# Attention closes, swap and peak, and the sample's distance table: three moves in the order of a hybrid decoder step

## The reference

```
h = rmsnorm(x);  proj = h @ w_in
qkv = silu(short_conv(proj[:, :1536]));  q, k = l2norm(q), l2norm(k)
o_a = rmsnorm(gated_delta_rule(q, k, v, g, beta, s0)) * silu(z_a)     # 4 heads of 128, in chunks
o_b = merge(window 128 step 1, window 512 step 4, window 2048 step 16) * silu(z_b)   # 8 heads of 64
y = rmsnorm(x + concat(o_a, o_b) @ w_out)
```

## Time and profile before

| | us |
|---|---|
| median of 3 runs | 1913.91 |
| lowest, highest | 1909.18, 1929.31 |
| the profiled execution | 1917.42 |
| its span | 1915.7 |
| TensorE busy in the span | 1731.0 (90%) |
| VectorE, ScalarE, GpSimd busy | 830.4, 640.2, 370.9 |

### The profile page before, as it was taken

How to read it: one execution, slowest core, us unless ns; L and a number is a source line. 1 busy time by engine, 2 the same in 40 slices (tenths; PEclk the granted TensorE clock), 3 DMA queues, 4 the chain that set the end, 5 groups by cost and what they waited for, 6 DMA issues and landing times. The chain is left out here.

```text
span 1915.7 us, 27681 instructions
## 1 busy us (share of the span) xinstructions
PE 1731.0 (90%) x9686; PEld 1420.9 (74%) x9686; DVE 830.4 (43%) x1913; ACT 640.2 (33%) x1550; POOL 370.9 (19%) x372
## 2 busy tenths in 40 slices
PE   5999999999999999977799899899988578889896
PEld 5998878888888888865688778778876546667674
DVE  3435413522351153127854544444442565445552
ACT  4534312421231132111425445444534223333331
POOL 0000000000000010026132422342243333423321
PEclk9999999999999999989799999999989569899998
DMA  5424677776566877769857457645430486465650
GB/s 171 121 67 100 167 232 217 146 180 236 145 177 203 216 160 154 237 212 290 225 132 194 121 124 158 163 114 122 133 111 15 147 235 190 150 169 171 187 180 27
DMA packets 228267, 311.30 MB, mean 162 GB/s; under 512 B 62973, under 2 KB 176509, under 8 KB 218669
## 3 DMA queue, kind: packets, MB, share of 16 engines
q1 hardware_dynamic: 223540, 301.35, 58.6%
q10 hardware_dynamic: 4608, 8.39, 1.3%
HBM read 229.10 MB, written 147.56 MB: 197 GB/s over the span
## 5 line engine op out<-in xcount | busy, mean ns | idle before, releaser
L399 PE MATMUL pj<-hT_hi,w_hi 128*128 128x512 f32 x896 | 362.5, 405 | 1.8 <-DVE raw L652 1.8
L400 PE MATMUL pj<-hT_lo,w_hi 128*128 128x512 f32 x896 | 355.2, 396 | 0.0
L401 PE MATMUL pj<-hT_hi,w_lo 128*128 128x512 f32 x896 | 354.8, 396 | 0.0
L401 PEld LDWEIGHTS pj<-hT_hi,w_lo 128*128 128x128 f32 x896 | 168.8, 188 | 41.0
L399 PEld LDWEIGHTS pj<-hT_hi,w_hi 128*128 128x128 f32 x896 | 168.9, 188 | 39.8 <-issue 2.1
L400 PEld LDWEIGHTS pj<-hT_lo,w_hi 128*128 128x128 f32 x896 | 169.2, 189 | 37.0
L1483 PE MATMUL o_ps<-pt,vt 128*65 128x256 f32 (+3 forms) x560 | 150.3, 391 | 10.7 <-DVE ot L1749 6.6
L1584 ACT ACTIVATE pt<-pt_ps 128x512 f32<-128x512 f32 x144 | 84.9, 590 | 153.6 <-PE pt_ps L1461 153.5
L2360 PE MATMUL y_bank<-wo_hi,mh 128*128 128x512 f32 (+1 forms) x272 | 114.9, 422 | 6.8 <-POOL ml L2345 4.6
L2361 PE MATMUL y_bank<-wo_lo,mh 128*128 128x512 f32 (+1 forms) x272 | 112.5, 414 | 0.0
L2362 PE MATMUL y_bank<-wo_hi,ml 128*128 128x512 f32 (+1 forms) x272 | 112.3, 413 | 0.0
(11 more groups left out here) (453 smaller groups left out, 3505.6 us busy)
## 6 DMA issues: line engine op xcount, KB each, us to landing
out_dram<-in_cache_k_win_dram SPq DMA_DIRECT2D x56, 584.0 KB, 8.4
out_dram<-in_cache_v_win_dram SPq DMA_DIRECT2D x56, 584.0 KB, 8.6
w_raw<-in_w_in_dram SPq DMA_DIRECT2D x31, 512.0 KB, 12.9
kq_all<-sil SPq DMA_DIRECT2D x32, 256.0 KB, 6.1
wqk<-hi SPq DMA_DIRECT2D x32, 256.0 KB, 5.8
wqk<-lo SPq DMA_DIRECT2D x32, 256.0 KB, 5.6
sc_class<-kq_all SPq DMA_DIRECT2D x16, 512.0 KB, 7.1
qs<-wqk SPq DMA_DIRECT2D x16, 512.0 KB, 7.4
```

The costliest lines, as they stand in the source:

```text
L399: pe.matmul(out, w_hi[s][:, k, :], hT_hi[:, k, cols], start=(k == 0), stop=False)
L400: pe.matmul(out, w_hi[s][:, k, :], hT_lo[:, k, cols], start=False, stop=False)
L401: mm = pe.matmul(out, w_lo[s][:, k, :], hT_hi[:, k, cols], start=False, stop=(k == KT - 1))
```

## The change

In `head_order` the costs change and swap and peak move: spread weighs 0 in place of 10, mix 12 and mix 16 weigh 0 and mix 17 weighs 18 in place of 8, close 0 and 1 weigh 4 each in place of 0, swap weighs 0 and peak 26 in place of 10 each, and peak follows swap at once, behind mix 16, in place of mix 17. (In head 7 spread, swap and peak don't exist, and mix 16 keeps its 8.)

The sample's table of distances is built in `project`, in tile 24, into `g_row`, stored with the masks one tile later (25), and comes with `kept_masks`, which grows by 48 columns. In `sample` TensorE transposes the old rows `stc` ahead of the product of the decay and ahead of the table.

```diff
-        pair, s_upto, s_after, s_own = (g_row[:, a:z] for a, z in zip(KEPT_AT, KEPT_AT[1:]))
+        pair, s_upto, s_after, s_own, win = (g_row[:, a:z] for a, z in zip(KEPT_AT, KEPT_AT[1:]))
+        far_at, win_a, win_b = (g_row[:, a:a + WIN] for a in range(KEPT + WALK, KEPT + WALK + 3 * WIN, WIN))
...
-                if t == TABLES_AT[2] + 4:
+                if t == TABLES_AT[2] + 5:
                     sp.wait_ge(masks_made, 1)
+                    sp.wait_ge(win_step, 16)
                     sp.dma_start(D.masks, g_row[:, 0:KEPT + WALK]).then_inc(masks_out, 16)
...
             then(pool.memset(g_row[:, 0:KEPT + WALK], 1.0))
+            SQ = DEC_SEQ * DEC_SEQ
+            for x, (at, step) in enumerate(((512, -DEC_SEQ), (NEAR_W - P, 0), (0, 0))):
+                pool.iota(far_at[:, SQ * x:SQ * x + SQ].bitcast(I32), pattern=[[1, DEC_SEQ], [-1, DEC_SEQ]], base=at, channel_multiplier=step).then_inc(far_done, 1)
...
+                if t == TABLES_AT[2] + 4:
+                    dve.wait_ge(far_done, 3)
+                    window_table(dve, win, far_at.bitcast(I32), win_a, win_b, win_step)
...
         if more and k == UNITS:
-            add(10, "spread")
+            add(0, "spread")
         if k >= LAG:
             m = k - LAG
-            add(8, "mix", m)
+            folds = more and m == UNITS - LAG
+            add(0 if m == 12 or folds else 18 if m == 17 else 8, "mix", m)
             if m < 8 and m % 2:
                 add(0, "near", m // 2)
-            if more and m == UNITS - LAG:
-                add(10, "swap")
-            if more and m == UNITS - 1:
-                add(10, "peak")
+            if folds:
+                add(0, "swap")
+                add(26, "peak")
             if m in (12, 17):
                 for r in (0, 1) if m == 12 else (2, 3):
-                    add(0, "close", r)
+                    add(4 if m == 12 else 0, "close", r)
...
+            pe.wait_ge(E.stc_in, 16)
+            for t in range(3 * NJ):
+                mm = pe.transpose(bank[0][:, 24 * t:24 * t + 24], stc[:, P * t:P * t + P], ident[0:24, 0:24])
+            mm.then_inc(G["stc_turned"], 1)
             pe.wait_ge(G["gm"], 1)
             pe.matmul(bank[6][0:NS, 0:H * NS], E.s_after, flat(sgm[:]), start=True, stop=True).then_inc(G["decay"], 1)
             pe.wait_ge(G["wide_tab"], 3)
...
-            pe.wait_ge(E.stc_in, 16)
-            for t in range(3 * NJ):
-                mm = pe.transpose(bank[0][:, 24 * t:24 * t + 24], stc[:, P * t:P * t + P], ident[0:24, 0:24])
-            mm.then_inc(G["stc_turned"], 1)
...
-            dve.wait_ge(G["far_at"], 3)
-            window_table(dve, t_win[:], far_at[:], t_a[:], t_b[:], G["win_step"])
             for x in range(3):
-                of = t_win[:, T * T * x:T * T * x + T * T].rearrange("p (t j) -> p j t", j=T)
+                of = E.win[:, T * T * x:T * T * x + T * T].rearrange("p (t j) -> p j t", j=T)
```

More of the change, by code:

```diff
@@ L163, in project @@
         tail_done, tail_stored, raw_head = sem("tail_done"), sem("tail_stored"), sem("raw_head")
-        mask_step, masks_made, masks_out = sem("mask_step"), sem("masks_made"), sem("masks_out")
+        mask_step, masks_made, masks_out, far_done, win_step = (sem(n) for n in ("mask_step", "masks_made", "masks_out", "far_done", "win_step"))
         iota_done, table_step, table_done, tables_out = (sem(n) for n in ("iota_done", "table_step", "table_done", "tables_out"))
@@ L758 @@
 LEVELS = (16, 32, 64)
-KEPT_AT = (0, P, P + NS, P + 2 * NS, P + 2 * NS + DEC_BATCH)
+WIN = 3 * DEC_SEQ * DEC_SEQ
+KEPT_AT = (0, P, P + NS, P + 2 * NS, P + 2 * NS + DEC_BATCH, P + 2 * NS + DEC_BATCH + WIN)
 WALK_AT = (0, len(LEVELS) * P // 2, len(LEVELS) * P // 2 + NB)
@@ L799, in gate_tensors @@
     env.kept_masks = sb("kept_masks", [P, KEPT])
-    env.pair, env.s_upto, env.s_after, env.s_own = (env.kept_masks[0:n, a:z] for n, a, z in zip((P, NS, NS, NS), KEPT_AT, KEPT_AT[1:]))
+    env.pair, env.s_upto, env.s_after, env.s_own, env.win = (env.kept_masks[0:n, a:z] for n, a, z in zip((P, NS, NS, NS, P), KEPT_AT, KEPT_AT[1:]))
     env.s_beta, env.s_egc, env.s_dl = (sb(n, [NS, H]) for n in ("s_beta", "s_egc", "s_dl"))
@@ L1891, in sample @@
         stc, st = sb("stc", [DEC_BATCH * TAIL, CONV_CH]), sb("st", [P, DEC_BATCH, H, P])
-        far_at = sb("far_at", [P, 3 * T * T], I32)
-        t_win, t_a, t_b = (sb(n, [P, 3 * T * T]) for n in ("t_win", "t_a", "t_b"))
         wide_tab = sb("wide_tab", [P, 3, T, SW_HEADS, T])
@@ L1900, in sample @@
             "r_made y1 vd attn_mm o_made o_squared o_eps o_pow o_scaled o_turned delta_gated su su_read st_stored "
-            "far_at win_step wide_tab tab_turned tab_copied step w_hi lsum_in inverted linv_stored".split())}
+            "wide_tab tab_turned tab_copied step w_hi lsum_in inverted linv_stored".split())}
         w_in, w_lo = ([sem(f"s_{n}{u}") for u in range(2)] for n in ("w_in", "w_lo"))
@@ L1950, in then @@
                 pool.wait_ge(G["tables"], n[0])
-            part = lambda x: far_at[:, T * T * x:T * T * x + T * T]
-            pool.iota(part(0), pattern=[[1, T], [-1, T]], base=NEAR, channel_multiplier=-T).then_inc(G["far_at"], 1)
-            pool.iota(part(1), pattern=[[1, T], [-1, T]], base=NEAR_W - P, channel_multiplier=0).then_inc(G["far_at"], 1)
-            pool.iota(part(2), pattern=[[1, T], [-1, T]], base=0, channel_multiplier=0).then_inc(G["far_at"], 1)
             then(pool.memset(x2[:], 0.0))
```

## The result

The kernel before ran at 1913.58 us (median of 20 runs, 1905.45 to 1929.31), the changed one at **1926.07 us** (20 runs, 1919.15 to 1934.31). The ratio is 1.0051, 95% interval 1.0034 to 1.0068: slower by half a percent, some 10 us (6.5 to 13; the two medians lie 12.5 apart). The forecast was 1923, in a range of 1908 to 1933.

A forecast was written before the change was run, and what follows sets the result against it. TensorE was taken to set the pace, busy 60.5 of a head's 66.0 us. Mixers +12.6 and sample -3.8 made +8.8 us: 1926.2 for the profiled execution, 1923 for the median, range 1908 to 1933.

The forecast's parts named there:

- Part 1: Heads 1 to 6: ks 1 goes before mix 12, so mix 13 waits less; gain 0.86 us a head.
- Part 2: Heads 1 to 6: turn_o 0, moved behind score 14, waits for GpSimd's norm; loss 1.3 us a head.
- head 7: Last head of the mixers: turn_o waits 2.3 us for norm 0 and av 1 comes later; loss 2.6 us.
- Part 3: End of a head: spread behind su 1, swap and peak before av 1 delay the exponentials; loss 1.28 us a head.
- The sum: Mixers in all: 9.6 us for heads 1 to 6, 0.4 for head 0, 2.6 for head 7, together +12.6 us.
- (c): Rival, chance 0.12: new pauses in each head lower TensorE's clock, adding 9 + 3 us, to 1935.
- Head 0: First head of the mixers: swap and peak ahead of ks 1 cost 0.4 us, between -0.2 and +1.2.
- the signs that the prediction named: Expected in the changed profile: named waits, heads of 67.7 us, silu 3 to 4 us sooner; wrong if the clock drops otherwise.
- Part 4: Sample stage: table built in the projection and old rows transposed first bring silu sooner; -3.8 us, between 2.5 and 4.2 gained.
- (a): Rival, chance 0.13: both new waits in the mixers are absorbed and the closes' gain stays; 1904 us.
- (b): Rival, chance 0.2: only one of the two new waits in the mixers is real; no change, 1914 us.
- (d): Rival, chance 0.05: the projection's mask or the larger table disturbs the projection's end; up to 3.9 us more.

The follow-up runs named there:

- Ks first: The order of before with ks 1 alone moved ahead of mix 12 in heads 1 to 6, plus the table in the projection: 0.9962 of the kernel before.
- the pause filled: Eight useless identity products on TensorE before the wait for the first exponential: 1.0043 on the changed kernel, 0.9937 on the closes around ks 1.
- the order alone: The kernel before with the new `head_order` and the sample stage as before: 1.0065 of the kernel before.
- the closes around ks 1: Old order, table in the projection, ks 1 between close 0 and close 1 (head 7: solve 1 between them): 0.9945 of the kernel before.

## Why the prediction was right

**Part 1** held closely: 0.88 a head for 0.86, mix 13's wait 0.79 for 0.8. Ks first has it without the new waits, at 7.3 us with the sample's gain (0.0038 of the time, 1.3 to 13 by its interval; 0.88 x 6 = 5.3 and 3.3 make 8.6). The steps that slip one place between the first exponential and ks 0 cost nothing, as assumed: with the pause filled and the clock whole this stretch takes 31.95 to 32.12, and 32.02 was its shortest before.

**Part 2** held: turn_o 0 waits 1.47 for GpSimd's norm, and the stretch grew by 1.28 where 1.3 was worked out. In the stretch, moving it back returned exactly that. In head 7 its wait is 2.17 (2.3 forecast), and av 1, on which the end hangs, starts 24.22 us after the pair mix 7 and ks 0 begins (1459.16 to 1483.38) where it started after 21.84 (1451.52 to the earlier trace rows): 2.4 for the 2.6 forecast. Head 7 as a whole took 68.9 to 74.7 us in the executions above, by its clock and whatever the order, so these 2.4 are read from a timeline and not proved by a time.

**Part 3** had the mechanism and was a little too large: 1.11 us a head for 1.28. Counted from qs 1, av 1 starts at 4.49 where 4.5 was worked out (swap at 3.99 for 4.1; the 0.49 by which swap is late is in the profile as a wait of 0.33). The terms that were a little too large are behind swap: peak starts at 4.69 for 4.8 and the sum of av 1 at 5.84 for 6.0. Before, this sum followed av 1's start by 1.24; now it follows by 1.35, so peak's place ahead of it costs about 0.1. The chain of peak, the sum, the squares and the exponentials is there as forecast, but nearly all of the loss is in the late start of av 1, by spread (0.6) and by swap (0.4).

**The sum** of the mixers, +12.6, met the 12.5 of the order alone, and that is partly luck. The waits of heads 1 to 6 gave 9.1 for 9.6. The same heads took 417.0 to 417.6 in three executions and 401.4 and 405.3 in two of the old order: 12 to 16 more. The 3 to 7 us beyond the waits go with the granted clock, 0.93 to 0.98 in place of 0.95 to 1.00, which the forecast left to its rival (c). Of that rival the mechanism is real, at 3 to 7 us in place of its 9 + 3. Against it head 7, with its 2.4 us of new waiting, was no longer than before: 74.3 and 68.9 us in the two of the old order, at granted clocks of 0.81 and 0.88, and 70.1 to 72.0 in the three of the new, at 0.86 to 0.89. Head 0, put at +0.4, took 77.6 us before and 76.7 to 78.9 in the changed order, so that term is not resolved. Two of the signs that the prediction named therefore point against it: the heads are 68.0 to 71.0 us and not 67.7 (with the pause filled and the clock whole they are 67.3 to 67.7), and the clock did drop otherwise than before.

**Part 4** was put at -3.8 and came to -3.3 at silu, -3.0 for the stage. Two steps of it failed. The bound that was named, the load of the old rows, took 0.88 of the 3.25. And the activation's table load was taken to stay where it was, done 10.8 after the stage's start; it stands behind ScalarE's copies of the table of distances, and these behind the transposes that the old rows now precede, so that it was over at 11.7 and became what silu waits for. Against this the seven steps of the convolution all took 0.56, as worked out.

For the convolution and GpSimd the Trainium skill, "SBUF — State Buffer", section "SBUF: two separate sides", was weighed: a lock that the first to start holds for its whole instruction. Three rows of this case agree with it. The addition of 1510.28, begun 0.29 ahead of GpSimd's subtraction (1510.57 for 2.47), kept its 0.56; the one begun 0.46 behind it took 2.58; the squares at 1512.70, of 0.43 otherwise, took 0.62 and ended 0.28 behind the subtraction's end.

In the projection the sixteen steps cost nothing, as forecast: VectorE does them from 746.05 to 749.69, and TensorE has no new wait up to the end of the stage.

**The rivals.** (a) and (b), one or both new waits absorbed, are out: both waits are in the trace, and ks first shows what the time is without them, 17 us lower. (c) came in part, as said. (d), a disturbed end of the projection, is not in the trace: TensorE's longest wait there is 8.2 us in both kernels.

## What to carry to other kernels

A wait that is shortened is worth only what the next queue lets through: close's 1.65 us gave 0.88 one way and 1.05 another, and the last 0.60 stood at a GpSimd step that had been ready 0.13 us ahead of its reader and moved by less than its reader did. A step moved ahead of another also carries its predecessors on every engine, and a list that is expanded from costs moves steps that nobody named; here turn_o did the larger harm. Of the versions tried, the old order with the closes around ks 1, and the table in the projection, has the lowest times: 0.9945 of the kernel before, 0.9937 with the pause filled. Both are faster than the kernel before beyond their intervals; against each other and against ks first (0.9962) they are not told apart.

## What the runs showed that was not expected

The low clock behind a pause depends on the order of the steps and repeats: two executions of the changed order have the same six periods within 0.1 us and the same six clocks, and a third the same sum. The pause of 2.2 us is followed by 3 to 10.5 us at 0.50 in all heads 1 to 6 of these three. TensorE's shorter wait of 1.5 us for GpSimd is followed by some 3.5 us at 0.50 in 15 of 36 heads, where without the wait none of 24 has them. Three stops of 0.4, 1.8 and 1.1 us within 7 us were followed by up to 24 us. Filling the long pause with useless products kept the clock at 1.00 in half of the heads or more without costing time there; over the whole kernel the gain was not resolved.
